# A two-layer decoder trunk on one core: one chunk order for both layers, residual and last down chunk moved into the gate chunks, the MLP's gating moved up, and 256-column products put behind 512-column ones

## What is computed

```python
for i in range(DEPTH):                                    # DEPTH = 2
    mix = token_mixer(x, positions, w_in[i], ...)         # see below
    x = layer_norm(DN_ALPHA * x + mix, ln1_g[i], ln1_b[i])
    ple = jax.nn.sigmoid(x @ w_ple_gate[i]) * (p[i] @ w_ple_proj[i])
    x = layer_norm(DN_ALPHA * x + conv_ffn(x, w_up[i], conv_w[i], conv_b[i], w_down[i]) + ple, ln2_g[i], ln2_b[i])

# token_mixer: proj = x @ w_in (17,408 columns), three dilated window attentions and one retention on its parts
merged = sigmoid(gate_a) * (attn @ w_attn_proj) + sigmoid(gate_r) * (ret @ w_ret_proj)
return merged @ w_out

# conv_ffn: h = x @ w_up (5,632 columns), causal convolution over three tokens per column, gate and up its halves
return (gelu(gate) * up) @ w_down
```

## Time and profile before

| | us |
|---|---|
| median of three runs (range) | 1577.38 (1577.19 to 1578.86) |
| the profiled execution, own time | 1578.85 |
| its span, first to last instruction | 1577.0 |
| PE busy, share of the span | 1522.4, 97% |
| PE weight loads busy | 1377.7, 87% |
| DVE busy | 964.2, 61% |
| ACT busy | 780.2, 49% |
| POOL busy | 38.8, 2% |
| DMA: bytes, mean rate | 265.83 MB, 169 GB/s |
| mean granted clock of PE | 0.993 of full |

### The profile page before, as it was taken

The page is one execution under the profiler, slowest core; times in us unless marked ns, Lnnn a source line. Parts: engine busy times, 40 slices in busy tenths (PEclk is TensorE's granted clock), DMA queues, the critical chain, the costliest instruction groups (busy, mean ns, idle before and its releaser), DMA issues.

```text
span 1577.0 us, 22960 instructions
## 1 busy us (share of the span) xinstructions
PE 1522.4 (97%) x9714; PEld 1377.7 (87%) x9714; DVE 964.2 (61%) x1075; ACT 780.2 (49%) x831; POOL 38.8 (2%) x23
## 2 busy tenths in 40 slices
PE   8999999999999999999899999999999999999986
PEld 8989989899888888887789999999998887988875
DVE  5564563645655667777765646556365557577776
ACT  5454453544644455555444645546455454455552
POOL 0000000000000010000000000000000001000000
PEclk9999999999999999999899999999999999999999
DMA  8544445455456465555445444454444554645540
GB/s 277 190 144 153 158 137 185 139 164 172 141 180 214 148 213 176 180 177 187 160 145 176 160 161 151 144 187 154 157 149 156 187 189 172 214 160 193 208 157 27
DMA packets 231478, 265.83 MB, mean 169 GB/s; under 512 B 4192, under 2 KB 221792, under 8 KB 230880
## 3 DMA queue, kind: packets, MB, share of 16 engines
q1 hardware_dynamic: 231248, 264.44, 50.4%
q10 hardware_dynamic: 144, 0.13, 0.0%
HBM read 263.50 MB, written 1.05 MB: 168 GB/s over the span
## 4 chain that ended last, share of the span: by engine, by line
PE 69%; DVE 18%; ACT 7%; issue 6%; DVEq 1%; ACTq 0%; DMA 0%; SPq 0%
PE bank L1179 15%; PE bank L1181 15%; PE bank L1180 15%; PE bank L1205 10%; DVE w_lo L702 9%; PE bank L1207 5%; ACT w_hi L373 4%; DVE scratch L1050 3%; ACT scratch L604 1%; PE acc L1314 1%; PE acc L1179 1%; PE acc L1335 1%; PE acc L1181 1%; PE acc L1180 1%; DVE scratch L1062 1%
## 5 line engine op out<-in xcount | busy, mean ns | idle before, releaser
L702 DVE TENSOR_TENSOR w_lo<-raw,w_hi 128x2048 fp32r<-128x2048 f32 x241 | 550.2, 2290 | 408.8 <-ACT w_hi L373 408.5
L373 ACT ACTIVATE w_hi<-raw 128x2048 fp32r<-128x2048 f32 x243 | 461.1, 1906 | 157.7 <-PE bank L1181 108.7
L1179 PE MATMUL bank<-xT_both,w_hi 128*128 128x256 f32 x1312 | 373.5, 285 | 0.0
L1180 PE MATMUL bank<-xT_both,w_hi 128*128 128x256 f32 x1312 | 371.2, 283 | 0.0
L1181 PE MATMUL bank<-xT_both,w_lo 128*128 128x256 f32 x1312 | 371.1, 283 | 0.0
L1205 PE MATMUL bank<-xT_both,w_hi 128*128 128x512 f32 x928 | 334.7, 403 | 16.3 <-DVE w_lo L702 14.7
L1207 PE MATMUL bank<-xT_both,w_lo 128*128 128x256 f32 x928 | 261.8, 282 | 0.0
L1180 PEld LDWEIGHTS bank<-xT_both,w_hi 128*128 128x128 f32 x1312 | 251.7, 192 | 0.6
L1179 PEld LDWEIGHTS bank<-xT_both,w_hi 128*128 128x128 f32 x1312 | 251.6, 192 | 0.6
L1181 PEld LDWEIGHTS bank<-xT_both,w_lo 128*128 128x128 f32 x1312 | 251.7, 192 | 0.0
L1205 PEld LDWEIGHTS bank<-xT_both,w_hi 128*128 128x128 f32 x928 | 176.0, 190 | 64.3 <-issue 13.9
(11 more groups left out here) (165 smaller groups left out, 1671.2 us busy)
## 6 DMA issues: line engine op xcount, KB each, us to landing
raw<-w_in SPq DMA_DIRECT2D x135, 1024.0 KB, 5.1
raw<-w_up SPq DMA_DIRECT2D x44, 1024.0 KB, 5.1
raw<-w_down SPq DMA_DIRECT2D x20, 1024.0 KB, 5.4
raw<-w_ret_proj SPq DMA_DIRECT2D x16, 1024.0 KB, 5.2
raw<-w_attn_proj SPq DMA_DIRECT2D x8, 1024.0 KB, 5.2
raw<-w_out SPq DMA_DIRECT2D x8, 1024.0 KB, 4.8
raw<-w_ple_gate SPq DMA_DIRECT2D x8, 1024.0 KB, 5.2
scratch<-ln_rows SPq DMA_DIRECT2D x4, 1024.0 KB, 7.5
```

The lines of the kernel that those rows point to most:

```text
L373: nc.scalar.activation(w_hi[:, s, :], raw[:, s, :], ACT.Copy).then_inc(hi_ready, 1)
L702: nc.vector.tensor_tensor(w_lo[:, s, :], raw[:, s, :], w_hi[:, s, :].bitcast(F32), ALU.subtract).then_inc(lo_ready, 1)
L1179: mm(dst, st_hi, mv_hi, start=start, stop=False)
L1180: mm(dst, st_hi, mv_lo, start=False, stop=False)
```

## The change

- `VALUES` is one tuple, that of layer 1. In layer 0 chunk 0 is now the first attention's values, 1 and 2 the retention's. Where the chunks 11 and 12 fall on the ring's last and first buffer (layer 0), `two_chunks` reads buffers 0 and 2, and the two chunks' columns are swapped in the loads. The places in ACT's, DVE's and PE's lists that hung on the layer hang on it no more.
- In the merge's round 0 PE waits for `ret_lo_ready` behind the first `w_ret_proj` chunk and `attend`, not ahead of them.
- The last round's `w_attn_proj` chunk is computed by `one_part`; ACT's copy and DVE's sum for it fall away, and DVE multiplies by the gate straight from PSUM.
- The residual is made in four parts of 512 columns, each behind the product of a sigmoid chunk. `last_hi`, `last_lo` and the two parts of the second up chunk come behind the third sigmoid chunk. The load of `last_raw` goes ahead of those of the first two up chunks.
- PE waits for bank 1 only before the first up chunk, and for bank 3 before the second.
- In the MLP DVE runs the product of `gated` ahead of `w_lo` of chunk 3, and `mid_low` between the `w_lo` of chunks 3 and 4. ACT takes the second half's `take_low` ahead of `gelu`. In the written-out tail `gated` and `take_centre` move up in the same way.
- In `both_parts` the eight 512-column products of a half of the chunk come first, then its eight 256-column ones.

The diff, without the lines that only drop `[l]` or carry the same step over:

```diff
-VALUES = ((0, 2, 12, (11, 14)), (1, 0, 11, (13, 14)))
+VALUES = (1, 0, 11, (13, 14))
...
-                    cols[v12 + u] = j * CH + (3 * (u + 1) + 2) * D
+                    cols[v12 + u] = j * CH + (3 * (u + 1 if slot(l, v12) < RING - 1 else 2 - u) + 2) * D
...
-                load(l, g, C_MLP, part(w_up, l, 0, KT, 0, CH))
-                load(l, g, C_MLP + 1, part(w_up, l, 0, KT, D_FF, CH))
                 sp.wait_ge(chunk_done, L0 + C_PLE + RING)
                 sp.dma_start(last_raw.rearrange("p (k n) -> p k n", k=2), part(w_down, l, 2 * NF - 2, 2, 0, D))\
                   .then_inc(last_loaded, 16)
+                load(l, g, C_MLP, part(w_up, l, 0, KT, 0, CH))
+                load(l, g, C_MLP + 1, part(w_up, l, 0, KT, D_FF, CH))
...
-                    if c == C_PLE - 3:
-                        product_low(c, j, 1)
...
                     copy_out(L0, C_PLE + 2 + j, j, ple_sig, func=ACT.Sigmoid)
+                    if j == 2:
+                        act.wait_ge(last_loaded, 16 * (l + 1))
+                        nc.scalar.activation(last_hi, last_raw, ACT.Copy).then_inc(last_hi_ready, 1)
+                        to_hi(l, L0 + C_MLP, R0 + 16 * C_MLP // RING, 1)
...
                     take_centre(0, value(i + 1))
+                    take_low(g, 3, 1, n)
                     gelu(value(l * NF + i + 1))
-                    take_low(g, 3, 1, n)
                     take_centre(1, value(i + 1))
...
-                    low_sum(prod_sum, j, 1, 3)
-                    gated_product(prod_a, j, 1).then_inc(products_ready, 1)
-                    dve.wait_ge(products_ready, l * NJ + j + 1)
+                    if j < NJ - 1:
+                        low_sum(prod_sum, j, 1, 3)
+                        gated_product(prod_a, j, 1).then_inc(products_ready, 1)
+                        dve.wait_ge(products_ready, l * (NJ - 1) + j + 1)
+                    else:
+                        dve.wait_ge(chunk_done, L0 + C_PLE - 3 + 1 + RING)
+                        nc.vector.tensor_tensor(prod_a.rearrange("p (a b) -> p a b", a=2), pair[1][:, :, 0:SEQ],
+                                                sig[:, 0, :].rearrange("p (a b) -> p a b", a=2), ALU.mult)\
+                          .then_inc(bank_read[2], 1)
+                        dve.wait_ge(bank_read[2], l * USES[2] + U_MERGE[2] + 2 * j + 3)
...
                       .then_inc(ple_ready, 1)
+                    dve.wait_ge(ple_ready, l * NJ + j + 1)
+                    x = X[:, :, j * CH:(j + 1) * CH]
+                    nc.vector.scalar_tensor_tensor(out=x, in0=x, scalar=ALPHA, in1=v,
+                                                   op0=ALU.mult, op1=ALU.add).then_inc(residual_ready, 1)
+                    if j == 2:
+                        dve.wait_ge(last_hi_ready, l + 1)
+                        nc.vector.tensor_tensor(last_lo, last_raw, last_hi.bitcast(F32), ALU.subtract)\
+                          .then_inc(last_lo_ready, 1)
+                        to_lo(l, L0 + C_MLP, 1)
...
                 def steady(g, i):
+                    gated(value(l * NF + i))
                     to_lo(l, g, 3)
+                    mid_low(value(nm + i + 1), 0)
                     to_lo(l, g, 4)
-                    gated(value(l * NF + i), value(nm + i + 1))
                     up_sum(0, value(i + 1))
...
-                dve.wait_ge(ple_ready, (l + 1) * NJ)
-                nc.vector.scalar_tensor_tensor(out=X[:, :, :], in0=X[:, :, :], scalar=ALPHA, in1=ple,
-                                               op0=ALU.mult, op1=ALU.add).then_inc(residual_ready, 1)
-                dve.wait_ge(last_hi_ready, l + 1)
-                nc.vector.tensor_tensor(last_lo, last_raw, last_hi.bitcast(F32), ALU.subtract)\
-                  .then_inc(last_lo_ready, 1)
                 turn = l * NF + NF - 3
+                gated(turn)
                 to_lo(l, L0, TAIL + 1)
+                mid_low(nm + NF - 2, 0)
                 to_lo(l, L0, TAIL + 2)
-                gated(turn, nm + NF - 2)
                 up_sum(0, NF - 2)
                 to_lo(l, L0, TAIL + 3)
                 taps(0, NF - 2)
                 up_sum(1, NF - 2)
+                taps(1, NF - 2)
+                gated(turn + 1)
                 to_lo(l, L0, TAIL + 4)
-                taps(1, NF - 2)
-                gated(turn + 1, nm + NF - 1, slot=1)
+                mid_low(nm + NF - 1, 1)
...
                         mm(pair[p][:, m, :], hi[:, o:o + P], src[:, k0 + k, :, :].rearrange("p a t -> p (a t)"),
                            start=first and k == 0, stop=False)
+                    for k in range(KT):
+                        o = k * CH + m * P
                         ins = mm(pair[p][:, m, SEQ:2 * SEQ], lo[:, o:o + P], src[:, k0 + k, 0, :],
                                  start=False, stop=last and k == KT - 1)
...
-                s = slot(l, c)
+                both = slice(slot(l, c), slot(l, c) + 2) if slot(l, c) < RING - 1 else slice(0, RING, RING - 1)
...
-                    if j and c == 1 - l:
+                    if j and c == 0:
                         transpose_ret(it, (bank[3], acc[3]))
                         transpose_prob(it2)
...
-                pe.wait_ge(ret_lo_ready, (l + 1) * NJ)
                 pair_free(0, U_MERGE[0] + 1)
                 both_parts(l, L0, g + 2, 0, ret, 0, last=False)
                 attend((l + 1) * NJ)
+                pe.wait_ge(ret_lo_ready, (l + 1) * NJ)
...
-                    attended(g + 9, j)
+                    if j < NJ - 1:
+                        attended(g + 9, j)
+                pair_free(1, U_MERGE[2] + 2 * NJ - 1)
+                one_part(l, L0, C_PLE - 3, 1, attn)
...
-                for b in (1, 3):
-                    pe.wait_ge(bank_read[b], l * USES[b] + U_MLP[b] + 1)
+                pe.wait_ge(bank_read[1], l * USES[1] + U_MLP[1] + 1)
                 up(g, 0, 0, 0)
+                pe.wait_ge(bank_read[3], l * USES[3] + U_MLP[3] + 1)
                 up(g, 1, 1, 0)
```

More of the change, by code:

```diff
@@ L295, in _ @@
                 if l == 0:
-                    load(l, 0, 1, part(w_in, 0, 0, KT, RV0 + CH, CH))
-                    load(l, 0, 2, part(w_in, 0, 0, KT, 2 * D, CH))
+                    load(l, 0, 1, part(w_in, 0, 0, KT, RV0, CH))
+                    load(l, 0, 2, part(w_in, 0, 0, KT, RV0 + CH, CH))
                     load(l, 0, 3, part(w_in, 0, 0, KT, 0, CH))
@@ L467, in mixer @@
                             nc.scalar.activation(rv_hi[:, t, :], bank[c % 3][:, :], ACT.Copy).then_inc(rv_hi_ready, 1)
-                    if not l and j and c == 1:
-                        finish_ret(l, j - 1, it, (bank[3], acc[3]))
                     if c == v0:
@@ L659, in _ @@
                 steady(L0 + C_MLP + (NF - 4) * 3, R0 + 16 * C_MLP // RING + (NF - 4) * 16, NF - 4)
-                act.wait_ge(last_loaded, 16 * (l + 1))
-                nc.scalar.activation(last_hi, last_raw, ACT.Copy).then_inc(last_hi_ready, 1)
                 turn = l * NF + NF - 2
@@ L904, in mixer @@
                         to_lo(l, g, c + 2)
-                    if l and j and c == 1:
+                    if j and c == 1:
                         finish_ret(j - 1, it)
@@ L919, in mixer @@
                                                     ALU.subtract).then_inc(bank_read[c % 3], 1)
-                    if not l and j and c == 1:
-                        finish_ret(j - 1, it)
                     if c == 9:
@@ L1057, in taps, with gated @@
                     ins.then_inc(conv_ready, 1)
-                def gated(turn, nm, slot=0):
+                def gated(turn):
                     dve.wait_ge(conv_ready, 2 * turn + 2)
@@ L1108, in _ @@
                 taps(1, NF - 1, whole=True)
-                gated(turn + 2, nm + NF, slot=2)
+                gated(turn + 2)
+                mid_low(nm + NF, 2)
                 n = n2 + 1
-                dve.wait_ge(residual_ready, l + 1)
+                dve.wait_ge(residual_ready, NJ * (l + 1))
                 if l < DEPTH - 1:
@@ L1238, in two_chunks @@
                                         xT_hi[:, k, t * P:(t + 1) * P], xT_lo[:, k, t * P:(t + 1) * P],
-                                        w_hi[:, s:s + 2, k * CH:(k + 1) * CH], w_lo[:, s:s + 2, k * CH:(k + 1) * CH],
+                                        w_hi[:, both, k * CH:(k + 1) * CH], w_lo[:, both, k * CH:(k + 1) * CH],
                                         k == 0, k == KT - 1)
```

37 lines of the change are left out of this document (17 added, 20 removed).

## The result

The changed kernel takes 1535.12 us (median of four runs, 1533.60 to 1536.32) where the kernel before takes 1577.41 (1577.19 to 1578.86): a ratio of 0.9729, with a 95% interval of 0.9713 to 0.9746. The profiled execution took 1534.09 us, its span is 1532.3. Against them stand 1534.5, worked out for the profiled execution, and 1533.5, forecast for the median.

What follows compares the result with a forecast made beforehand. PE was taken as the bound, busy 1522.4 of 1577.0 us; gains of 5.8, 2.1, 3.6, 2.5 and 30.3 (both MLPs) sum to 44.3 off 1578.85, so 1534.5, and 1533.5 for the median; range 1527 to 1547.

Steps and rivals of the forecast that it cites:

- One chunk order: Layer 0's last three mixer rounds: 297.7 us instead of 303.5, 5.8 less; reading buffers 0 and 2 together costs 0.
- The wait for `ret_lo` and the merge's end: Both layers' merges: the wait for `ret_lo` goes, 2.1 us less; the second `mid` comes sooner at the end, 2.5 less.
- 256 behind 512 in the merges: Merge chunks: grouping products by width takes 5.56 us a chunk, 0.095 less in each of 2 x 19, 3.6 in all.
- The sigmoid chunks at nothing: Work moved into the sigmoid chunks before the MLP is hidden in idle time of DVE and ACT: cost 0.
- The first round: MLP's first round: PE idles 3.1 us before the fourth up chunk, where it idled 1.12.
- The fall of the clock: Rival: half clock behind the new 3.1 us pause in each MLP, +3.4 to +6.8 us, 1537 to 1540; chance 0.23.
- the forecast's own case: The MLP's first-round pause of 3.1 us brings no half clock; 1533.5 us in all, chance 0.45.
- The steady rounds: Seven MLP rounds a layer: bound by PE at 16.8 us each instead of 17.30.
- the loop some 0.25: Steady MLP rounds: some 0.25 us of each round put down to the loop, besides PE's products and idle time.
- The tail: MLP's tail: 30.0 us from the ninth round's start to the third down product, before 40.5; PE idles 2.1.
- The slower rival: MLP rounds: a loop through three engines doesn't outrun PE, so the 3.1 us pause recurs every round; 1601 us, chance 0.03.
- Sum: Whole kernel: all terms, 44.3 us less than the profiled 1578.85, give 1534.5; the median 1533.1, rounded up to 1533.5.

Runs made afterwards that it cites:

- Experiments seven and eight: Changed kernel with the `gelu` table loaded early: 1531.26 us; the same plus the fourth up chunk's two parts made earlier in the MLP's first round: 1525.78 us.
- experiment ten: Changed kernel with two more DVE operations at the end of each steady MLP round: 1567.54 us, ratio 0.9930 to the kernel before.
- the gating kernel: Kernel before with only `gated`, `mid_low`, `take_low` and `take_centre` moved as in the change: 1555.04 us, ratio 0.9848.
- experiment eleven: Kernel before with one more DVE operation at the end of each steady MLP round: 1614.79 us, ratio 1.0235.

## Why the prediction was right, point by point

**One chunk order.** Right in place and size: 5.85 in the trace, 5.2 by itself, for 5.8. That the ring's first and last buffer cost nothing to read together was right too.

**The wait for `ret_lo` and the merge's end.** 2.3 and 2.5 for 2.1 and 2.5. The pause at the end is 0.15 us, where some 0.3 was left by my working.

**256 behind 512 in the merges.** The mechanism was right, the term mis-sized: 2.4 us instead of 3.6, 0.06 a chunk instead of 0.095. The step that failed is putting 0.01 for the changes of width that are left in a chunk, and the plain 0.227 and 0.120 for all products between them. Two up chunks behind one another in a round, the first behind a down chunk:

```profile
610.14 1.98 PE L1212 MATMUL bank<-xT_both,w_hi 128*128 128x512 f32 x8
611.96 1.11 PE L1216 MATMUL bank<-xT_both,w_lo 128*128 128x256 f32 x8
612.91 2.00 PE L1212 MATMUL bank<-xT_both,w_hi 128*128 128x512 f32 x8
614.75 1.12 PE L1216 MATMUL bank<-xT_both,w_lo 128*128 128x256 f32 x8
```

The row of eight behind other 512-column products takes 1.82 us, 0.227 each. The row behind 256-column ones takes 1.84: by the starts inside it its products stand 0.234, 0.235, 0.229, 0.232 and 0.231 us apart, and only then 0.227, and the first 256-column product behind it takes 0.113 instead of 0.120. So a change of width there and back costs 0.02 in this order, and a chunk with two of them takes 5.59 us, not 5.56. Alternating it takes 5.65. That is 0.06 won in most chunks of the merges and in the second up chunk of a round, and 0.08 in a chunk behind other 512-column products. In the merge's first round the three chunks behind products of 128 columns or behind `attend` take 5.67 or 5.68.

The Trainium skill (TensorE: Matmul & The Clock Gate, Back-to-back issue gap) gives the gap of an isolated matmul at full clock as N/2.4 + 2.5 ns by its own width; for streams it names measured figures instead, 131 ns at 512 columns, which no row of this case comes near (0.22 us and more). By the formula, taking the order back would have changed nothing; it cost 4.5 us, in a kernel in which the instructions are the same. The measurement decides: the order in which widths follow each other has a price here.

**The sigmoid chunks at nothing.** Right: PE waits nowhere among the first three up chunks.

**The first round.** 3.00 us for 3.1, through the chain as it was written down. The fall of the clock, which I had as a rival at 0.23 and priced at 3.4 us or more, came with it: two falls of 3.41 us, but only 1.3 us lost in each, since the half clock begins inside the pause. So the forecast's own case, a pause without a fall, did not happen, and the rival's time, 1537 to 1540, wasn't reached either. Experiments seven and eight show both shares.

The Trainium skill (ScalarE: Activation LUTs, What ACT_TABLE_LOAD costs) puts a switch of tables at 1283 ns for the load and some 1380 ns for a drain, 2.66 us. The trace agrees on the load, 1.28 us; a drain it doesn't show: the load ends at 591.02 and the `gelu` begins at 591.03. And moving the load out of the chain shortened the pause by 1.1 us, less than the load itself, not by 2.66.

**The steady rounds.** Better than worked out, 16.61 for 16.8. The step that failed is "the loop some 0.25". I had it as what was left of 17.30 when products and visible idle time are taken away; but it was wait. Idle time in the trace is counted from the modelled end of a matmul, which lies later than the next one's start would: a 512-column product is shown as 0.39 us long, and the next starts 0.227 behind it. With the products at 16.79 without a pause, the old round of 17.30 held 0.51 us of wait, where its window shows 0.29 idle. Over 14 rounds 0.19 each is 2.7 us that I hadn't counted.

**The tail.** 29.86 for 30.0, with 1.74 us of idle time where 2.1 stood. With the half clock gone behind it, the whole of the two MLPs came to 15.4 and 15.1 us for 15.2 and 15.1. That agreement is partly luck: the clock's 1.3 us a layer, left out, and the rounds' 1.3, not counted, cancel.

**The slower rival.** The loop doesn't bind: rounds are 16.61 with an operation more in each, and it does bind with two. In experiment ten's row of DVE such an operation takes 2.2 us from start to start. So the working of some 28 us over two rounds was good enough to decide it (28 + 2 x 2.2 = 32.4 is under two rounds, 33.2; 28 + 4 x 2.2 = 36.8 is over, and two rounds of experiment ten take 37.1). By experiment ten the mechanism exists; what I expected of it there was too low, by the hand-overs.

**Sum.** The span's gain is 44.7, and the forecast's 44.3 has three errors in it: 1.2 too much for the merges, 2.6 for the clock left out, 2.7 too little for the rounds. They leave 1.1 us, which the 1.2 at the start (of the execution, not of the change) and tenths in the other terms make good. That three errors of 1 to 3 us nearly cancel is luck, the mechanisms apart. The step from 1534.5 to 1533.1, since the median of the kernel before lay 1.47 below its profiled execution, did not carry over: here the median lies 1.03 above it.

## What to carry to other kernels

When one engine is the bound and the others have room in the mean, write down the closed chain over the engines for one round, and move what the next round's first operand needs to the front of it: that alone won 23.5 us here, most of it in the tails, where the whole change won 42.3, and afterwards 2 us of added work a round cost nothing. Then look at the first round of the loop by itself, since its list has work (a table load, a copy of a chunk that is already there) which the steady rounds don't have in that place; a pause there is paid twice, in time and in clock. And take the price of an instruction from a row in which the same things stand ahead of it: the same 512-column product in the same routine costs 0.227 or up to 0.235 us by what the row before it was.

## What the runs showed of the hardware that was not expected

- **The fall of the clock is not set by the length of a pause alone.** Behind pauses of 3.00 us in the changed kernel PE went to 1.2 GHz in both layers; behind 2.93 us in layer 0 of the gating kernel it didn't, and behind 2.91 in its layer 1 it did. Over the six profiled kernels with such a pause it fell behind 9 of 12 pauses of 2.9 to 3.0 us. In the control kernel of experiment eleven it fell behind 5 of 9 of 2.4 to 2.5 us, with the table load moved behind one of two of 1.9 us, and in experiment ten behind none of 1.7. The falls lasted 3.41 us, or 6.83 (layer 1 of the gating kernel, layer 0 of experiment ten). What decides it stays open.
- **Half clock is free where another chain sets the pace.** In experiment eleven a round with a fall in it and a round without one both take 19.51 us.
- **The start varies.** PE's 41st product starts at 13.8 to 15.9 us in the five profiles of kernels with the old chunk order, and at 14.0 to 15.4 in the eight with the new one. Of a gain of 1.2 us in this stretch in one pair of profiles nothing can be said to come from the change.
- **A 512-column product costs more behind 256-column ones, and the rise lasts for five products**: 0.229 to 0.235 us each, then 0.227. Grouping the widths wins 0.06 us a chunk in the merges (2.4 / 38) and 0.18 a round.
